# Two float16 gate parts in place of three bfloat16 parts, summed in PSUM

## The reference

```python
expert = i1 * N_SUBKEYS + i2
gate = jax.nn.softmax(best_v, axis=-1).astype(h.dtype)
...
u = jnp.take(u_tab, ex, axis=0)
act = jax.nn.gelu(jnp.einsum('thkd,td->thk', u, hx), approximate=False) * gx
vv = jnp.take(v_tab, ex, axis=0)
return jnp.einsum('thk,thkd->td', act, vv)
```

## Time and profile before

| | |
|---|---|
| median of 3 runs | 2172.35 us (2169.05 to 2172.98) |
| profiled execution, its span from the first to the last instruction | 2164.7 us; the page gives no other time of it |
| TensorE matmul | 2097.8 us busy, 97% |
| VectorE | 1574.3 us, 73% |
| ScalarE | 1049.4 us, 48% |
| GpSimd | 378.4 us, 17% |
| mean granted TensorE clock | 0.991 of full speed |
| HBM read | 332.54 MB, mean 154 GB/s |

### The profile page before, as it was taken

The page is one execution under the profiler, slowest core; times in us unless marked ns, Lnnn a source line. Parts: engine busy times, 40 slices in busy tenths (PEclk is TensorE's granted clock), DMA queues, the critical chain, the costliest instruction groups (busy, mean ns, idle before and its releaser), DMA issues.

```text
span 2164.7 us, 50057 instructions
## 1 busy us (share of the span) xinstructions
PE 2097.8 (97%) x19768; PEld 1894.7 (88%) x19768; DVE 1574.3 (73%) x2866; ACT 1049.4 (48%) x1801; POOL 378.4 (17%) x182
## 2 busy tenths in 40 slices
PE   8999999999999999999899999999999999999997
PEld 7888999999888988888688889999998889888885
DVE  6655897788788559955576558958887784698555
ACT  5544445444544444455455444454444554444443
POOL 0022699100000000000001236990000000000000
PEclk9999999999999999999999999999999999999998
DMA  6212355444444554455342134454444445444551
GB/s 265 94 46 100 135 177 191 158 154 149 168 170 173 194 175 149 161 194 194 131 144 96 43 122 146 180 182 151 153 156 169 167 170 197 170 150 162 193 194 67
DMA packets 46619, 335.07 MB, mean 155 GB/s; under 512 B 5168, under 2 KB 5296, under 8 KB 6320
## 3 DMA queue, kind: packets, MB, share of 16 engines
q1 hardware_dynamic: 46512, 333.61, 43.0%
HBM read 332.54 MB, written 1.05 MB: 154 GB/s over the span
## 4 chain that ended last, share of the span: by engine, by line
PE 85%; issue 5%; POOL 4%; DVE 4%; ACT 1%; DMA 1%; POOLq 0%; SPq 0%; ACTq 0%
PE PS L1650 33%; PE PS L1621 28%; PE PS L1295 9%; PE PS L1639 4%; POOL low L433 3%; PE PS L1311 3%; PE PS L1488 1%; PE PS L1521 1%; PE PS L1635 1%; PE PS L1532 1%; DMA ring<-in_w_slabs 1%; ACT high L457 1%; PE PS L1343 1%; PE PS L1394 0%; DVE low L796 0%
## 5 line engine op out<-in xcount | busy, mean ns | idle before, releaser
L648 ACT CAST high<-ring 128x1024 fp32r<-128x1024 f32 x512 | 535.9, 1048 | 553.1 <-PE PS L1621 435.6
L1621 PE MATMUL PS<-hTh,high 128*128 128x256 f32 x2048 | 588.5, 287 | 9.2 <-ACT GA L652 3.4
L1621 PE MATMUL PS<-hTl,high 128*128 128x256 f32 x2048 | 577.3, 282 | 0.0
L1621 PE MATMUL PS<-hTh,low 128*128 128x256 f32 x2048 | 577.0, 282 | 0.0
L1061 DVE TENSOR_TENSOR low<-ring,high 128x1024 fp32r<-128x1024 f32 x416 | 506.7, 1219 | 26.3 <-ACT high L648 18.1
L1621 PEld LDWEIGHTS PS<-hTh,high 128*128 128x128 f32 x2048 | 385.9, 188 | 13.8 <-issue 6.7
L1621 PEld LDWEIGHTS PS<-hTl,high 128*128 128x128 f32 x2048 | 386.1, 189 | 1.3
L1621 PEld LDWEIGHTS PS<-hTh,low 128*128 128x128 f32 x2048 | 385.8, 188 | 0.0
L1650 PE MATMUL PS<-high,WH 128*128 128x512 f32 x1024 | 322.6, 396 | 0.0
L1650 PE MATMUL PS<-low,WH 128*128 128x512 f32 x1024 | 316.2, 390 | 0.0
L1650 PE MATMUL PS<-high,WL 128*128 128x512 f32 x1024 | 315.4, 389 | 0.0
(11 more groups left out here) (258 smaller groups left out, 2931.6 us busy)
## 6 DMA issues: line engine op xcount, KB each, us to landing
ring<-in_peer_slabs SPq DMA_DIRECT2D x256, 1024.0 KB, 4.8
ring<-in_w_slabs SPq DMA_DIRECT2D x58, 1024.0 KB, 4.8
xres<-in_x SPq DMA_DIRECT2D x2, 512.0 KB, 4.4
out<-obuf SPq DMA_DIRECT2D x2, 512.0 KB, 2.6
cst<-in_consts SPq DMA_DIRECT2D x1, 680.0 KB, 10.2
praw<-in_p_t SPq DMA_DIRECT2D x1, 512.0 KB, 14.9
gfin<-in_g_final SPq DMA_DIRECT2D x1, 512.0 KB, 5.7
vec<-in_vecs SPq DMA_DIRECT2D x1, 356.0 KB, 7.1
```

What stands on the lines that cost most here:

```text
L648: act.copy(high[:, (c0[L] + j) % DEEP], ring[:, place, half * D:(half + 1) * D]).then_inc(part_hi, 1)
L1621: ins = mm(PS[:, 6 + j % 2, 0:SEQ], u[:, b, ks], h[:, k], start=n == 0, stop=n == 3 * KT - 1)
```

## The change

A gate is multiplied with 2^15 (`GATE_UP`) when ScalarE takes it out of PSUM (line 691), then split into two float16 parts in place of three bfloat16 parts. `hot1`, `hot2`, `is_i2`, `decoded`, `repeats` and `iota_half` become float16. All three chunks now use two matmuls for each token, which accumulate in PSUM, of 48, 32 and 48 columns. `sum_gates`, `gate_sum` and the semaphore `gates_summed` go. `apply_gates` reads PSUM in all three chunks and multiplies with 2^-15 in the same operation.

```diff
+GATE_UP = 2.0 ** 15
...
-        hot2 = place("hot2", R + 22528, [2, 3, GROUP, WIDEST], BF16)
+        hot2 = place("hot2", R + 22528, [2, 2, GROUP, WIDEST], F16)
...
-                    act.copy(repeats[:, b], decoded[:, :, tokens].unsqueeze(3).broadcast_to([P, 5, GROUP, REP])).then_inc(repeated, 1)
+                    act.copy(repeats[:, b], decoded[:, :, tokens].unsqueeze(3).broadcast_to([P, 4, GROUP, REP])).then_inc(repeated, 1)
...
-                        act.copy(gate_T[:], PS[:, 5, 0:SEQ]).then_inc(slot_T, 1)
+                        act.activation(gate_T[:], PS[:, 5, 0:SEQ], ACT.Identity, scale=GATE_UP).then_inc(slot_T, 1)
...
                 link(dve.tensor_copy(decoded[:, 2], gate_T[:]))
-                link(dve.tensor_tensor(gate_rest[:], gate_T[:], decoded[:, 2], ALU.subtract))
-                link(dve.tensor_copy(decoded[:, 3], gate_rest[:]))
-                dve.tensor_tensor(decoded[:, 4], gate_rest[:], decoded[:, 3], ALU.subtract).then_inc(parts_made, 1)
+                dve.tensor_tensor(decoded[:, 3], gate_T[:], decoded[:, 2], ALU.subtract).then_inc(parts_made, 1)
...
-                                      is_i2[:, b, :, 0:width].rearrange("p t (a c) -> p t a c", c=REP).unsqueeze(1).broadcast_to([P, 3, GROUP, width // REP, REP]),
-                                      repeats[:, b, 2:5].unsqueeze(3).broadcast_to([P, 3, GROUP, width // REP, REP]), ALU.mult).then_inc(hots_made, 1)
+                                      is_i2[:, b, :, 0:width].rearrange("p t (a c) -> p t a c", c=REP).unsqueeze(1).broadcast_to([P, 2, GROUP, width // REP, REP]),
+                                      repeats[:, b, 2:4].unsqueeze(3).broadcast_to([P, 2, GROUP, width // REP, REP]), ALU.mult).then_inc(hots_made, 1)
...
-                    if chunk == 1:
-                        dve.wait_ge(gates_summed, NGROUPS * (L - 1) + 1 + g)
-                        dve.tensor_tensor(acts, acts, gate_sum[:], ALU.mult).then_inc(gated, 1)
-                    else:
-                        dve.wait_ge(spread_ps, g0 + 1 + g)
-                        dve.tensor_tensor(acts, acts, PS[:, 4 + b, 0:GROUP * width].rearrange("p (t i) -> p i t", t=GROUP), ALU.mult).then_inc(gated, 1)
-
-                def sum_gates(g, b):
-
                     dve.wait_ge(spread_ps, g0 + 1 + g)
-                    dve.tensor_reduce(gate_sum[:], PS[:, 4 + b].rearrange("p (t q i) -> p i t q", t=GROUP, q=2), AX.X, ALU.add).then_inc(gates_summed, 1)
+                    dve.scalar_tensor_tensor(acts, acts, 1 / GATE_UP, PS[:, 4 + b, 0:GROUP * width].rearrange("p (t i) -> p i t", t=GROUP), ALU.mult, ALU.mult).then_inc(gated, 1)
...
                     split_uv(s + 1, j + 1, 0)
-                    sum_gates(s + NGROUPS, j % 2)
                     split_uv(s + 1, j + 1, 1)
...
-                        if chunk == 1:
-                            at = 2 * t * width
-                            mm(PS[:, 4 + b, at:at + 2 * width], hot1[:, b, t], hot2[:, b, 0:2, t, 0:width], start=True, stop=False, skip_group_check=True)
-                            ins = mm(PS[:, 4 + b, at + width:at + 2 * width], hot1[:, b, t], hot2[:, b, 2, t, 0:width], start=False, stop=True, skip_group_check=True)
-                            continue
-                        for part in range(3):
-                            ins = mm(PS[:, 4 + b, t * width:(t + 1) * width], hot1[:, b, t], hot2[:, b, part, t, 0:width], start=part == 0, stop=part == 2)
+                        for part in range(2):
+                            ins = mm(PS[:, 4 + b, t * width:(t + 1) * width], hot1[:, b, t], hot2[:, b, part, t, 0:width], start=part == 0, stop=part == 1)
```

More of the change, by code:

```diff
@@ L9 @@
 F32R = mybir.dt.float32r
-BF16 = mybir.dt.bfloat16
+F16 = mybir.dt.float16
 U32 = mybir.dt.uint32
@@ L150, in hybrid_encoder @@
         cst = place("cst", 14336, [NCONST])
-        gate_sum = place("gate_sum", 16016, [WIDTHS[1], GROUP])
         vec = place("vec", 16400, [DEPTH, NVEC])
@@ L162, in hybrid_encoder @@
         zeros = place("zeros", R + 25088, [P])
-        iota_half = place("iota_half", R + 25216, [NSUB], BF16)
+        iota_half = place("iota_half", R + 25216, [NSUB], F16)
         praw = place("praw", R + 24064, [DEPTH, 2, SEQ])
@@ L213, in hybrid_encoder @@
         WL = place("WL", R + 20992, [2, SEQ], F32R)
-        hot1 = place("hot1", R + 21504, [2, GROUP, NSUB], BF16)
-        hot2 = place("hot2", R + 22528, [2, 3, GROUP, WIDEST], BF16)
[L216 to L219, removed]
+        hot1 = place("hot1", R + 21504, [2, GROUP, NSUB], F16)
+        hot2 = place("hot2", R + 22528, [2, 2, GROUP, WIDEST], F16)
+        is_i2 = place("is_i2", R + 23680, [2, GROUP, WIDEST], F16)
+        decoded = place("decoded", R + 24064, [4, SEQ], F16)
+        repeats = place("repeats", R + 24704, [2, 4, GROUP, REP], F16)
         gate_T = place("gate_T", R + 19968, [SEQ])
@@ L287, in hybrid_encoder @@
         parts_made, repeated = sem("parts_made"), sem("repeated")
-        is_i2_made, hots_made, spread_ps, gates_summed, gated = (sem(n) for n in ("is_i2_made", "hots_made", "spread_ps", "gates_summed", "gated"))
+        is_i2_made, hots_made, spread_ps, gated = (sem(n) for n in ("is_i2_made", "hots_made", "spread_ps", "gated"))
         ga_ready, w_hi, w_lo, peer_ps = (sem(n) for n in ("ga_ready", "w_hi", "w_lo", "peer_ps"))
```

## The result

The changed kernel takes 2140.85 us (2139.81 to 2142.32, 4 runs) against 2170.7 us (2167.53 to 2172.98, 4 runs) for the kernel before: a ratio of 0.9862, interval 0.9849 to 0.9875. Measured once more beside other versions, it was 2142.44 against 2171.64 us, 0.9863 (0.9838 to 0.9888). The forecast was 2144.5 us. The profiled execution is 2138.0 us long from first to last instruction, 26.7 us less than the one before.

The account below looks back on a forecast made before the run. TensorE was taken as the bound, its matmul row busy for 97% of the span. Savings of 26.4 + 1.7 - 0.2 = 27.9 us gave 2164.7 - 27.9 + 7.65 = 2144.5 us, range 2138 to 2151.

Parts of the forecast that it names:

- First chunk: First chunk's spread: eight of 24 matmuls go in each group at 25.8 ns, 0.207 us a group, all on the chain.
- Second chunk: Second chunk's spread: still 16 matmuls, eight narrowed from 64 to 32 columns; 0.027 us a group, 1.7 us in all.
- rival that columns count: Spread of 32-column matmuls: each 32 columns fewer save 13 ns, 6.4 us in place of 1.7: 2139.8 us; chance 4%.
- Third chunk: Third chunk's spread: eight of 24 matmuls go in each group, 0.207 us; 26.4 us over 128 groups in two chunks.
- VectorE's lead: Last group's `WL` to the `spend` reading it: from 0.28 to -0.11 us, 0.1 us lost a layer, 0.2 in all.
- VectorE becomes the bound: Gates' product costs 65 ns more; VectorE's period 3.34 us against 3.235, 4.0 us lost in all: 2148.5 us; chance 10%.
- The sum: VectorE's 64 TENSOR_REDUCE in the middle chunk go, from iterations with 1.22 us idle: worth nothing.
- the start of the gates: Before the first spread, two VectorE operations of 128x256 go and ScalarE's scaled evacuation replaces a copy: worth nothing.
- `repeats`: On ScalarE, shrinks from 320 to 256 elements; ScalarE waits for TensorE in every period: worth nothing.
- the transfers: No DMA added or moved; the ring must deliver 157 and 162 GB/s, and gives 194 GB/s without spreads.
- float16: VectorE products and TensorE weights keep their bfloat16 durations; rivals of lost rate, 2270 or 2400 us, get 3% for both.
- What lies around a span: Whole kernel: the median, 2172.35 us, stands 7.65 us above the profiled span of 2164.7 us; added to the forecast.

Follow-up runs that it names:

- side-by-side version: Changed kernel, second chunk's spread as 8 matmuls of 64 columns writing both float16 parts, halves summed on VectorE: 2131.88 us, ratio 0.981; again 2130.64 us, 0.9814.

## Why the prediction was right

The direction, the size and the mechanism came out: 27.9 us forecast, 27.7 us in the stretches. The medians are further apart, 29.9 and 29.2 us in the two comparisons, and the profiled executions less, 26.7 us. What these 1 to 2 us either way are is not settled, and runs of the kernel before spread by 12 us in one of them (2165.46 to 2177.69). Step by step:

*First chunk.* Forecast 31 x 0.207 = 6.4 us for the 31 periods, measured 7.28. The spread itself did as forecast, 0.62 to 0.41 us. The rest is a term I left out: before the change, each turn of TensorE's loop in this chunk (every fourth period) had about 3.09 us in the place of 2.94 for the 24 `hidden` matmuls, six times in the 31 periods of either layer, 6 x 0.15 = 0.9 us; after it all but one of the 31 take 2.93 us. In the chain of the kernel before:

```profile
425.13 0.62 PE PS L1639 x24
425.75 3.09 PE PS L1621 x24
428.85 0.62 PE PS L1639 x24
```

I had this row and took it as untouched. Where the cost went can be read from the instructions of the loop itself, though no run tests it. The loop's branch, before and after the change:

```profile
L1675 PEldq COMPARE_BRANCH  x1: 215/215/215, 439.6 to 439.6; - x1
```
```profile
L1657 PEldq COMPARE_BRANCH  x1: 207/207/207, 438.4 to 438.4; - x1
```

And TensorE's timeline around these two turns, the last spread of the turn and the first matmul of the next:

```profile
439.35 0.78 PE L1639 MATMUL PS<-hot,hot 128*128 128x48 bf16 x24
440.10 0.39 PE L1621 MATMUL PS<-hTh,high 128*128 128x256 f32 x1
```
```profile
438.49 0.57 PE L1621 MATMUL PS<-hot,hot 128*128 128x48 f16 x16
438.90 0.36 PE L1608 MATMUL PS<-hTh,high 128*128 128x256 f32 x1
```

TensorE's sequencer runs ahead of the matmuls. With a spread of 24 it came to the loop's end at 439.53 us, in the middle of the spread, whose last matmul started 0.41 us later; the first `hidden` matmul of the next turn followed only 0.57 us after that point, so there was a gap (0.16 us from the spread's last start, where 0.025 is usual). With a spread of 16 it came there before the spread's first matmul, 0.59 us ahead of its last one, and the gap is gone. The six turns of a layer all look like this in either kernel, but for one after the change that has a gap of 0.07 us.

*Second chunk.* Forecast 0.027 us a group, measured 1.00 / 30 = 0.033. The floor holds: 16 matmuls of 32 columns take 0.41 us, some 26 ns each, as 16 of 48 columns do. The rival that columns count is refuted, and the side-by-side version shows the other side of it: with half the matmuls, each twice as wide, 5.2 us a layer are won. The Trainium skill's page "TensorE: Matmul & The Clock Gate" (section "Wait — 56ns, not 53.3ns?") gives about 25 ns as the least from start to start, however few the columns. The trace agrees, with some 26 ns here and 25.0 ns between 24 and 20 matmuls.

*Third chunk.* Forecast 6.4 us for the 31 periods, less 0.1; measured 5.37. This is the term that was over-sized: the row gives what a matmul occupies of the chain, and 31 x 0.03 us came back in the spend matmuls behind it. It nearly cancels the first chunk's surplus of 0.9 us a layer, by chance: the sum is closer than its terms.

*VectorE's lead.* Forecast: used up at the end (0.28 to -0.11 us), measured 0.9 us left. The `WL` of the last group of the chunk and the `spend` that reads it, for the earlier trace rows:

```profile
892.87 0.41 DVE L1144 TENSOR_TENSOR WL<-GA,WH 128x256 fp32r<-128x256 f32 x1
```
```profile
894.18 0.70 PE L1632 MATMUL PS<-high,WH 128*128 128x512 f32 x2
```

VectorE's period is 3.275 us, near the 3.27 forecast; TensorE's is 3.267, not 3.235, so it gains only 0.01 us a period, and the lead goes from 1.17 us to 0.91 in 30 periods. The forecast of a first wait for `WL` failed with the same term. That the two are this close was right, and two runs show it: with the product left at three parts nothing is won (0.9997), and with 65 ns more on the gates' product the rival "VectorE becomes the bound" happens, at 0.98 us a layer in place of the 2.0 I gave it, since TensorE's slower pace leaves it more lead.

*The sum, the start of the gates, `repeats`, the transfers, float16:* nothing, as forecast.

*What lies around a span.* I took 7.65 us. Runs that list both show 1.8 us (2142.44 and 2140.6 us; for the kernel before 2171.64 and 2169.9). The profiled execution was thus about 2166.5 us, a quick one, and the 7.65 us were mostly its distance to the median. The forecast used it only to get back to that median, so no error came of it. The median of the kernel before has since moved from 2172.35 to 2170.7 us with a fourth run; that is 1.65 of the 3.65 us between the forecast time and the measured one.

## What to carry to other kernels

On a chain of small matmuls, count matmuls and not columns: one of 32 or 48 columns took some 26 ns here and one of 64 about 31, so one wide matmul and a sum on an engine that idles beat two narrow ones that accumulate. An engine that is busy all through a stage sets what a saving on the other is worth, even where no wait shows yet: compare the two periods, and the lead divided by their difference. And a row's duration prices what is removed, but not what its neighbours do afterwards; where a per cent of a stage matters, undo the edit in one stage alone and read that stage's length.

## What was unexpected

The pace of a matmul depends on what surrounds it, without any wait. Twelve `spend` matmuls of 512 columns take 2.85 us between spreads of 16 and 2.82 between spreads of 20 or 24; VectorE's, ScalarE's and the transfers' load (20 against 159 GB/s) and the form of the loop change nothing, with the granted clock at 1.00 all through. And the loop's turn in the first chunk cost 0.15 us with 24 matmuls in the spread and next to nothing with 16, as far as the traces tell because the matmuls handed over ahead of the branch last until it is done.
